# A hybrid RWKV-7/Mamba-2 step with a PEER layer: the mixer's triangular inverse on 64x64 blocks with a corner join, later k and r scores, and loop alignment without padding

## The chip, the cores and the metric

The kernel runs on one core of a Trainium2 chip. The metric is the device time of one execution in microseconds (us). The kernel before takes 2727.44 us, the median of 3 runs (2725.97 to 2730.17).

## The reference

One layer is applied to 576 tokens: 512 of a prompt and 64 of a sample stream, with a model width of 1024. `n = RMSNorm(x)`, `P = n @ W_in`; the columns of P go to eight RWKV-7 heads and eight Mamba-2 heads of 64 channels; `h = x + W_out [RWKV || Mamba]`; then `h = h + PEER(RMSNorm(h))`, and a last RMSNorm. The part that matters here is the RWKV recurrence, per head with a 64x64 state S:

```
def step(S, inp):
    r_t, w_t, k_t, v_t, a_t, b_t = inp
    sa = jnp.einsum('bhvk,bhk->bhv', S, a_t)
    S = S * w_t[:, :, None, :] + sa[..., None] * b_t[:, :, None, :] + v_t[..., None] * k_t[:, :, None, :]
    return S, jnp.einsum('bhvk,bhk->bhv', S, r_t)
```

PEER picks 128 experts for each token out of 16384 and applies them: `hid = x . u[e]`, `out = sum gelu(hid) * gate * v[e]`.

## The kernel before, in words

The program runs in stages: `project_in` (P), `mix` (both mixers), `project_out` and `route` (W_out, the expert keys and their ranking), `spread_gates` (gates as a dense table), `experts`, `finish`. Each stage is a block with one instruction stream for each engine, and the streams meet through semaphores. Names of engines in the profile: PE is TensorE, DVE VectorE, ACT ScalarE, POOL GpSimd, SP SyncE.

**The mixer** (`mix`, L593 to L1300). Tokens are taken in five tiles (`TILES`): four of 128 tokens, and the last of 64, the sample stream. In a tile the recurrence is solved in parallel form. A token's contribution `u` obeys (I - A) u = y, where A holds the scores a·b of every later token with every earlier one, strictly triangular, 128x128 for each of the eight heads. The kernel inverts the triangular matrix by doubling: level n (n = 1 to 6; 1 to 5 for 64 tokens, `last_level`, L524) joins diagonal blocks of 2^n into blocks of 2^(n+1). Heads are held in two halves e = 0, 1 of four heads q each, and for a half one level is:

- `q{n}{e}` (L859): four products of `mT` and `xx` (the inverse so far), 128x128 each.
- VectorE multiplies the bank by the level's mask into `pq` (L1239, tile name `level`).
- `x{n}{e}` (L865) and `t{n}{e}` (L866): four products each, `xt` with `pq` and `pq` with `xt`, the next inverse and its transpose; ScalarE copies the banks to `xx` and `xt` (`take`, L970; tile names `inv`, `invT`). On the last level only t is made.

A tile's steps are ordered by hand in `tile_parts` (L509). Every engine walks the same list and does what it has in each part; there is one order for each engine, and nothing overtakes. For a tile i the order is B1, L1, L2, ..., L6, B5, and between the levels stand parts of the next tile (A1 to A5, its preparation), of this tile's Mamba (Y1 to Y3) and of the tile before (C1 to C4, its output):

```
between = {1: ("C1", "Y1", "A1"), 2: ("C2", "A2", "Y2", "A2b"), 3: ("C3", "A3", "Y3"), 4: ("A4", "C4"), 5: ("A5",)}
```

B1 (L822 on TensorE) turns the four operands `bT`, `kT`, `aT`, `rT` and makes five pairs of scores (`scores`, L832): `ab` and `m` (the matrix and its transpose, which the levels need), then `ak`, `rb`, `rk`, which only B5 needs. VectorE in B1 (L1209 on): masks `ab` into `mT` and `m` into `xx` (L1220), adds the identity to `mT` and masks it into `xt`, half by half (L1229, L1230, SBUF to SBUF), then masks `ak` and `rb` (L1220). GpSimd adds the identity to `xx` (L1090), and masks `rk` (L1094), which ScalarE has copied. B5 (L892) makes y from the state and `ak`, u from y and `xt`, the output from `rb` and `rk`, and the new state; the next tile's B1 waits for that state.

Products go to eight PSUM banks in turn (`Banks`, L556, `mixer_jobs`, L529): a job may start when the job eight places ahead of it in the list has been taken. All numbers are four bytes wide; for one such product the trace holds two records of the weight load and two of the product.

In A3 VectorE does the key norm, `kk`, `tmp_a`, `b_hat` and `k_hat` (L1177 to L1183); in Y3 the Mamba state (L1265, L1267); in A4 eight operations on the Mamba segments (L1190) and a sum; in A1 ScalarE does a tanh and a sigmoid ahead of the products `w` and `a` (L780). GpSimd scales the outputs of the tile before in C3 (L718 to L722), makes the products of the bonus (L1079, L1080) and `xw` in A3, and does Mamba's norm in L5 (L1111).

**The experts** (`experts`, L1799). For TensorE each of 32 groups has 192 products for `hidden` (18 groups; the others were made ahead) and 192 for `out`, three products each with a split of the operands (`three_products`, L113). The groups are walked by `groups` (L1835 on): the first one, a loop over pairs, the 18th, and a second loop with seven turns of two groups. TensorE's stream alone is aligned: ahead of both loops stands `eng.addr_align(align)` (L1842, L1848) with `FETCH` = 256 instructions.

Of the kernel before, what the change touches and what calls it, by code (L numbers as in the profile page):

```python
# [32 lines left out]
P = 128  # L33
# [30 lines left out]
LEVELS = 7  # L64
# [14 lines left out]
C_MS, C_LT0, C_LEV = (P * n for n in range(6, 9))  # L79
C_DCOL = C_LEV + P * LEVELS  # L80
# [3 lines left out]
def shape_constants():  # L84
# [11 lines left out]
    c[:, C_MS:C_MS + P] = s < t  # L96
    for n in range(LEVELS):
        b = 1 << n
        m = ((s // (2 * b) == t // (2 * b)) & (s // b > t // b)) | (s == t)
        c[:, C_LEV + P * n:C_LEV + P * (n + 1)] = m if n else m & (s != t)  # L100
        if n == 0:
            c[:, C_LT0:C_LT0 + P] = m.T
# [406 lines left out]
def tile_parts():  # L509
    parts = [(name, 0) for name in ("A1", "A2", "A2b", "A3", "A4", "A5")]  # L510
    between = {1: ("C1", "Y1", "A1"), 2: ("C2", "A2", "Y2", "A2b"), 3: ("C3", "A3", "Y3"), 4: ("A4", "C4"), 5: ("A5",)}
    for i in range(NT):
        parts.append(("B1", i))
        for n in range(1, last_level(i) + 1):
            parts.append((f"L{n}", i))
            for name in between.get(n, ()):
                j = i + {"A": 1, "Y": 0, "C": -1}[name[0]]
                if 0 <= j < NT:
                    parts.append((name, j))
# [4 lines left out]
def last_level(i):  # L524

    return LEVELS - 1 if TILES[i][1] == P else LEVELS - 2


def mixer_jobs():  # L529
# [4 lines left out]
    for part, i in tile_parts():  # L534
# [6 lines left out]
                  + [(f"{name}{e}", "dve") for name in ("ab", "m", "ak", "rb") for e in range(2)]  # L541
                  + [("rk0", "act"), ("rk1", "act")],
# [3 lines left out]
        if part[0] == "L":  # L546
            n = int(part[1])
            one = [(f"q{n}{e}", "dve") for e in range(2)]
            for e in range(2):
                one += [(f"x{n}{e}", "act")] * (n < last_level(i)) + [(f"t{n}{e}", "act")]  # L550
# [42 lines left out]
def mix(core, params, om):  # L593
# [10 lines left out]
    with ExitStack() as ctx:  # L604
# [13 lines left out]
        mT, ak, rb, rk = (sb(n, P, 2, 4, P) for n in ("mT", "akT", "rbT", "rkT"))  # L618
        xx, xt = sb("inv", P, 2, 4, P), sb("invT", P, 2, 4, P)
        pq = sb("level", P, 2, 4, P)  # L620
# [103 lines left out]
        with nc.Block() as block:  # L724
# [25 lines left out]
            def _(pe):  # L750
                pe.wait_ge(par_in, 7 * 16)
                pe.wait_ge(zeroed, 3)
# [68 lines left out]

                def b1(i, tok, T, rc, xc):  # L822
# [9 lines left out]
                    def scores(name, lhs, rhs):  # L832
                        o = [b.start(pe, f"{name}{e}", i) for e in range(2)]
                        for q in range(4):
                            for e in range(2):
                                es = slice(e * HD, (e + 1) * HD)
                                ins = pe.matmul(o[e][0:T, q * T:(q + 1) * T], lhs[es, q, 0:T], rhs[es, q, 0:T],
# [4 lines left out]
                    scores("ab", bT, aT)  # L842
                    scores("m", aT, bT)
                    b.wait_taken(pe, "rT", i)
                    scores("ak", kT, aT)
                    scores("rb", bT, rT)
                    scores("rk", kT, rT)
# [1336 lines left out]
```

## Time and profile before

| what | us | busy share or clock |
|---|---|---|
| median of 3 runs | 2727.44 | |
| the profiled execution's own time | 2724.83 | |
| its span, first to last instruction | 2722.8 | mean clock 0.952 |
| TensorE busy in the span | 2509.6 | 92% |
| VectorE busy | 1550.2 | 57% |
| ScalarE busy | 968.2 | 36% |
| GpSimd busy | 651.8 | 24% |

How to read it: the profile is one execution, so the sum of a change is made against its own 2724.83 us. The clock is the share of full speed that TensorE was granted; it has two levels, 1.00 (2.4 GHz) and 0.50 (1.2 GHz), and what stands between is a mean over a stretch. A busy TensorE is not TensorE at its peak, since its records overlap. A number in brackets behind a row of the timeline is the time in which the engine stood idle just before, with what ended it.

### The profile page before, as it was taken

What the parts mean: (1) busy time and instruction counts of PE and PEld (TensorE: products, weight loads), DVE (VectorE), ACT (ScalarE), POOL (GpSimd) and SP (SyncE); (2) the same over time, 40 slices, a digit from 0 to 9 for tenths busy, and PEclk for the clock granted to TensorE, in tenths of its full rate; (3) what the DMA queues carried; (4) which work ended last, traced back from release to release, by engine and by line L of the source; (5) the groups of instructions that cost most, each with busy time, mean ns of one, the idle gap of its engine ahead of it and who ended that gap; (6) DMA issues with size and microseconds to landing.
All of it is one profiled execution on the core that took longest, in us unless ns stands there. A gap on an engine that the chain in (4) does not pass through costs nothing. (4 is left out here: it accounts for less than half of the span.)

```text
span 2722.8 us, 48234 instructions
## 1 busy us (share of the span) xinstructions
PE 2509.6 (92%) x18910; PEld 2446.0 (90%) x18910; DVE 1550.2 (57%) x2800; ACT 968.2 (36%) x1818; POOL 651.8 (24%) x313
## 2 busy tenths in 40 slices
PE   7977888887899899899979999999999998999997
PEld 6976778787799899888879999999999998999997
DVE  4334554633678776677745454454554543677774
ACT  3335334422332232688853322322322221222222
POOL 2433343423254545111122211211211210000000
PEclk9997899868999899999989999999999999999999
DMA  5331000003233233366664323323323322454551
GB/s 182 114 106 41 24 24 1 13 1 128 65 98 96 90 102 102 115 181 191 193 209 150 112 94 110 112 94 110 112 94 110 112 94 78 153 175 158 191 174 40
DMA packets 162452, 296.11 MB, mean 109 GB/s; under 512 B 11873, under 2 KB 99233, under 8 KB 158121
## 3 DMA queue, kind: packets, MB, share of 16 engines
q1 hardware_dynamic: 162344, 294.61, 32.9%
q8 instruction: 76, 1.25, 0.2%
q14 instruction: 32, 0.25, 0.0%
HBM read 230.26 MB, written 64.31 MB: 108 GB/s over the span
## 5 line engine op out<-in xcount | busy, mean ns | idle before, releaser
L115 PE MATMUL banks<-w_high,v_high 128*128 128x288 f32 x2048 | 605.4, 296 | 12.0 <-issue 11.6
L117 PE MATMUL banks<-w_high,v_low 128*128 128x288 f32 x2048 | 605.6, 296 | 0.0
L116 PE MATMUL banks<-w_low,v_high 128*128 128x288 f32 x2048 | 604.3, 295 | 0.0
L115 PE MATMUL banks<-res_hi,u_high 128*128 128x288 f32 x1440 | 428.6, 298 | 11.7 <-ACTq L2004 10.9
L117 PE MATMUL banks<-res_hi,u_low 128*128 128x288 f32 x1440 | 425.7, 296 | 0.0
L116 PE MATMUL banks<-res_lo,u_high 128*128 128x288 f32 x1440 | 425.4, 295 | 0.0
L115 PEld LDWEIGHTS banks<-w_high,v_high 128*128 128x128 f32 x2048 | 385.2, 188 | 15.5 <-issue 11.8
L117 PEld LDWEIGHTS banks<-w_high,v_low 128*128 128x128 f32 x2048 | 385.3, 188 | 0.0
L116 PEld LDWEIGHTS banks<-w_low,v_high 128*128 128x128 f32 x2048 | 385.2, 188 | 0.0
L1998 DVE TENSOR_TENSOR res_x<-banks,res_x 128x288 f32<-128x288 f32 x512 | 225.4, 455 | 280.7 <-PE banks L117 280.7
L1618 POOL TENSOR_TENSOR u_low<-u_raw,u_high 128x1024 fp32r<-128x1024 f32 x72 | 183.6, 2551 | 707.1 <-ACT u_high L1614 707.1
L1892 ACT ACTIVATE v_high<-v_raw 128x1024 fp32r<-128x1024 f32 x128 | 135.3, 1059 | 473.2 <-PE banks L117 473.2
L115 PE MATMUL banks<-res_hi,q_wh 128*128 128x288 f32 x864 | 263.0, 304 | 32.4 <-POOL q_wl L199 22.6
L1969 DVE TENSOR_TENSOR gated<-gelu_out,gates_in 128x576 f32<-128x576 f32 x128 | 156.7, 1224 | 226.6 <-ACT gelu_out L1949 226.6
L115 PEld LDWEIGHTS banks<-res_hi,u_high 128*128 128x128 f32 x1440 | 271.5, 189 | 12.2 <-issue 12.1
L116 PEld LDWEIGHTS banks<-res_lo,u_high 128*128 128x128 f32 x1440 | 271.5, 189 | 0.0
L117 PEld LDWEIGHTS banks<-res_hi,u_low 128*128 128x128 f32 x1440 | 271.3, 188 | 0.0
L116 PE MATMUL banks<-res_lo,q_wh 128*128 128x288 f32 x864 | 260.2, 301 | 0.0
L117 PE MATMUL banks<-res_hi,q_wl 128*128 128x288 f32 x864 | 260.0, 301 | 0.0
L1974 DVE TENSOR_TENSOR w_low<-gated,w_high 128x576 fp32r<-128x576 f32 x128 | 191.4, 1495 | 54.2 <-ACT w_high L1941 54.2
L115 PEld LDWEIGHTS banks<-res_hi,q_wh 128*128 128x128 f32 x864 | 167.7, 194 | 37.4 <-POOL q_wl L199 24.6
L1896 DVE TENSOR_TENSOR v_low<-v_raw,v_high 128x1024 fp32r<-128x1024 f32 x128 | 156.6, 1225 | 43.3 <-ACT v_high L1892 43.3
(327 smaller groups left out, 4473.5 us busy)
## 6 DMA issues: line engine op xcount, KB each, us to landing
v_raw<-arg_v SPq DMA_DIRECT2D x128, 512.0 KB, 3.9
scratch_gates<-gate_stage SPq DMA_DIRECT2D x18, 2048.0 KB, 9.3
u_raw<-arg_u SPq DMA_DIRECT2D x36, 1024.0 KB, 5.8
gates_in<-scratch_gates SPq DMA_DIRECT2D x32, 1152.0 KB, 7.2
q_raw<-arg_u SPq DMA_DIRECT2D x38, 512.0 KB, 3.6
scratch_hidden<-gelu_ahead SPq DMA_DIRECT2D x56, 288.0 KB, 2.4
gelu_out<-scratch_hidden SPq DMA_DIRECT2D x56, 288.0 KB, 2.9
in_raw<-arg_w_in SPq DMA_DIRECT2D x25, 512.0 KB, 4.0
```

What stands on the lines that cost most here:

```text
L115: pe.matmul(out, ah, bh, start=first, stop=False)
L116: pe.matmul(out, ah, bl, start=False, stop=False)
L117: return pe.matmul(out, al, bh, start=False, stop=last)
L1618: pool.tensor_tensor(self.lo[:, jj % 2], self.raw[:, jj // 2, jj % 2], self.hi[:, jj % 2].bitcast(F32), ALU.subtract).then_inc(self.low, 1)
L1892: act.activation(vh[:, q], v_raw[:, q], ACT.Copy).then_inc(v_high, 1)
L1896: dve.tensor_tensor(vl[:, q], v_raw[:, q], vh[:, q].bitcast(F32), ALU.subtract).then_inc(v_low, 1)
L1969: dve.tensor_tensor(prod[:, jj % 2, :], gelu[:, jj % 2, :], gates[:, par, :, jj], ALU.mult).then_inc(prod_done, 1)
L1974: dve.tensor_tensor(wl[:, par, jj, :], prod[:, jj % 2, :], wh[:, par, jj, :].bitcast(F32), ALU.subtract).then_inc(w_low, 1)
L1998: dve.tensor_tensor(x, core.psum[:, 4 + k % 4, 0:HALF], x, ALU.add).then_inc(out_added, 1)
```

## The change

It does five things.

1. The inverse is built on the two 64x64 diagonal blocks of each 128x128 matrix, up to level 5: `mT`, `inv` (with `inv[:, e, 0]` the inverse and `inv[:, e, 1]` its transpose) and `pq` hold 64 columns for each head, masks of the levels are 64 columns wide, and a product is made for each block. Tokens 0 to 63 lie on partitions 0 to 63, the others on 64 to 127.
2. x and t of a half share one bank and one copy of 512 elements (256 of each). On level 5 ScalarE copies the blocks to where they are needed in three pieces (`last_blocks`).
3. Level 6 becomes `join`: the corner scores `al` (tokens of the first half with tokens of the second), kept in `mL`, times the first block's inverse, copied, times the second block's transposed inverse, copied into the corner of `xt` by ScalarE. There are four products of 64x64 for each half in either step. `xt` is zeroed once, on GpSimd.
4. The scores `ak`, `rb` and `rk` with their masks become parts of their own, S1 behind level 1, S2 behind level 2, S3 behind level 3.
5. The first alignment in `experts` skips its padding by a branch (`max_nops=0`), the second is removed.

The core of the diff:

```diff
-LEVELS = 7
+LEVELS = 6
+HALF_T = 64
...
-    between = {1: ("C1", "Y1", "A1"), 2: ("C2", "A2", "Y2", "A2b"), 3: ("C3", "A3", "Y3"), 4: ("A4", "C4"), 5: ("A5",)}
+    between = {1: ("C1", "Y1", "S1", "A1"), 2: ("C2", "A2", "Y2", "A2b", "S2"), 3: ("C3", "A3", "Y3", "S3"),
+               4: ("A4", "C4"), 5: ("A5",)}
...
-    return LEVELS - 1 if TILES[i][1] == P else LEVELS - 2
+    return LEVELS if TILES[i][1] == P else LEVELS - 1
...
+                def blocks(name, i, T, lhs, rhs):
+                    o = [b.start(pe, f"{name}{e}", i) for e in range(2)]
+                    for q in range(4):
+                        for e in range(2):
+                            es = slice(e * HD, (e + 1) * HD)
+                            for d in range(T // HALF_T):
+                                ds = slice(d * HALF_T, (d + 1) * HALF_T)
+                                ins = pe.matmul(o[e][ds, q * HALF_T:(q + 1) * HALF_T], lhs[es, q, ds], rhs[es, q, ds],
+                                                start=True, stop=True)
+                            if q == 3:
+                                b.finish(ins)
+
+                def by_block(o, T, lhs, rhs, at=0):
+                    for q in range(4):
+                        for d in range(T // HALF_T):
+                            ds = slice(d * HALF_T, (d + 1) * HALF_T)
+                            ins = pe.matmul(o[ds, at + q * HALF_T:at + (q + 1) * HALF_T], lhs[ds, q, :], rhs[ds, q, :],
+                                            start=True, stop=True)
+                    return ins
...
-                            four(f"q{n}{e}", i, T, lambda q: mT[0:T, e, q, 0:T], lambda q: xx[0:T, e, q, 0:T])
+                            b.finish(by_block(b.start(pe, f"q{n}{e}", i), T, mT[:, e], inv[:, e, 0]))
                         for e in range(2):
                             b.wait_taken(pe, f"q{n}{e}", i)
-                            if n > 1:
-                                b.wait_taken(pe, f"t{n - 1}{e}", i)
-                            if n < last:
-                                four(f"x{n}{e}", i, T, lambda q: xt[0:T, e, q, 0:T], lambda q: pq[0:T, e, q, 0:T])
-                            four(f"t{n}{e}", i, T, lambda q: pq[0:T, e, q, 0:T], lambda q: xt[0:T, e, q, 0:T])
+                            o = b.start(pe, f"x{n}{e}", i)
+                            by_block(o, T, inv[:, e, 1], pq[:, e])
+                            b.finish(by_block(o, T, pq[:, e], inv[:, e, 1], 4 * HALF_T))
...
+                def join(i, tok, T, rc, xc):
+                    lo, hi = slice(0, HALF_T), slice(HALF_T, P)
...
+                    for e in range(2):
+                        b.wait_taken(pe, f"al{e}", i)
+                        b.wait_taken(pe, f"x{LEVELS - 1}{e}", i)
+                        four_blocks(f"q{LEVELS}", e, hi, lambda q: mL[:, e, q, :], lambda q: inv[lo, e, 0, q, :])
+                    for e in range(2):
+                        b.wait_taken(pe, f"q{LEVELS}{e}", i)
+                        four_blocks(f"x{LEVELS}", e, lo, lambda q: pq[hi, e, q, :], lambda q: xt[hi, e, q, hi])
...
+                def last_blocks(name, i, e, T):
+                    o = b.get(act, name, i)[:, :].rearrange("p (x q t) -> p x q t", x=2, t=HALF_T)
+                    if T == P:
+                        act.activation(inv[0:HALF_T, e, 0], o[0:HALF_T, 0], ACT.Copy)
+                    for d in range(T // HALF_T):
+                        ds = slice(d * HALF_T, (d + 1) * HALF_T)
+                        ins = act.activation(xt[ds, e, :, ds], o[ds, 1], ACT.Copy)
+                    b.took(ins, name, i)
...
                 if align:
-                    eng.addr_align(align)
+                    eng.addr_align(align, max_nops=0)
                 with eng.Fori(0, NH // 2 - 1) as it:
...
                 whole(eng, NH - 1, 1, first=False, last=True)
-                if align:
-                    eng.addr_align(align)
                 with eng.Fori(0, (NG - NH) // 2) as it:
```

## Rows read from the trace of the kernel before

**Rows 1.** Stretches: us, busy PE, PEld, DVE, ACT, POOL, clock, DMA, GB/s
```profile
200.00:620.00 420.00, 345.32 (x2847) 311.83 (x2847) 208.73 (x363) 164.12 (x301) 146.33 (x113) 0.82 0.07 20
...
1393.00:2722.00 1329.00, 1291.31 (x9650) 1284.49 (x9648) 718.84 (x907) 350.35 (x483) 183.59 (x72) 0.99 0.36 122
```

**Rows 2.** Timeline, third tile, first level: start, us, engine, line
```profile
395.36 1.16 PE L837 MATMUL banks<-a_hatT,b_hatT 64*128 64x128 f32 x16 [0.44 <-ACT a_hatT L970]
...
396.55 1.29 DVE L1220 TENSOR_TENSOR mT<-banks,shape_constants 128x512 f32<-128x512 f32 x2 [2.70 <-PE banks L837]
...
403.81 1.64 DVE L1230 TENSOR_TENSOR invT<-mT,shape_constants 128x512 f32<-128x512 f32 x1
...
408.49 2.08 PE L769 MATMUL banks<-level,invT 128*128 128x128 f32 x8 [0.90 <-DVE level L1239]
...
401.52 3.38 POOL L1094 TENSOR_TENSOR rkT<-rkT,shape_constants 128x512 f32<-128x512 f32 x2
...
413.74 0.70 PE L873 MATMUL banks<-ssm_states,xbc_in 64*128 64x256 f32 x4
```

**Rows 3.** Timeline of the last tile (64 tokens), first level
```profile
561.28 1.12 PE L837 MATMUL banks<-a_hatT,b_hatT 64*64 64x64 f32 x16
...
566.10 0.99 DVE L1230 TENSOR_TENSOR invT<-mT,shape_constants 64x256 f32<-64x256 f32 x1
...
568.80 1.11 PE L769 MATMUL banks<-level,invT 64*64 64x64 f32 x8 [0.96 <-DVE level L1239]
```

**Rows 4.** Timeline of the third tile, level 2
```profile
420.51 1.95 PE L769 MATMUL banks<-inv,mT 128*128 128x128 f32 x16
...
426.03 1.90 PE L880 MATMUL banks<-xdt,segments 128*128 128x64 f32 x16
```

**Rows 5.** Timeline of the third tile, levels 3 and 4
```profile
431.51 2.05 PE L769 MATMUL banks<-inv,mT 128*128 128x128 f32 x16
...
443.73 2.08 PE L769 MATMUL banks<-level,invT 128*128 128x128 f32 x8 [3.88 <-DVE level L1239]
...
449.99 1.95 PE L769 MATMUL banks<-shape_constants,dA_rows 128*128 128x128 f32 x16
```

**Rows 6.** Timeline: third tile's level 5 and B5, fourth tile's scores
```profile
454.56 1.16 PE L769 MATMUL banks<-level,invT 128*128 128x128 f32 x8 [0.40 <-DVE level L1239]
...
461.96 1.06 PE L899 MATMUL banks<-s_mid_pairs,a_hatT 128*128 128x128 f32 x8
...
479.21 1.47 PE L837 MATMUL banks<-a_hatT,b_hatT 64*128 64x128 f32 x16
```

**Rows 7.** Timeline: weight loads of half and quarter array at both clocks
```profile
467.76 0.55 PEld L910 LDWEIGHTS banks<-v_tok,k_hat 128*64 128x64 f32 x16
...
533.35 1.00 PEld L769 LDWEIGHTS banks<-shape_constants,dA_rows 64*64 64x64 f32 x16
...
579.84 1.82 PEld L769 LDWEIGHTS banks<-inv,mT 64*64 64x64 f32 x16
```

**Rows 8.** DVE groups by form: the level mask of 256 elements
```profile
L1239 DVE TENSOR_TENSOR level<-banks,shape_constants 64x256 f32<-64x256 f32 x10 | 4.1, 413 | 5.9 <-PE banks L769 5.8
```

**Rows 9.** Stretches of the tensor engine: us, busy (records), granted clock
```profile
380.00:385.00 5.00, 5.00 (x48) 1.00 0.01 3
...
560.00:565.00 5.00, 4.95 (x82) 0.50 0.01 3
...
565.00:570.00 5.00, 3.09 (x43) 0.84 0.00 0
...
575.00:605.00 30.00, 29.89 (x254) 0.50 0.01 1
```

**Rows 10.** Timeline of PE around the entry of the experts' second loop
```profile
2311.97 0.60 PE L115 MATMUL banks<-w_high,v_high 128*128 128x288 f32 x1 [11.57 <-issue]
...
2312.37 0.44 PE L116 MATMUL banks<-w_low,v_high 128*128 128x288 f32 x1
...
2312.61 0.44 PE L117 MATMUL banks<-w_high,v_low 128*128 128x288 f32 x1
```

More of the change, by code:

```diff
@@ L78 @@
 C_ID, C_ONE, C_TRI, C_REV, C_DINC, C_DEXC = (P * n for n in range(6))
-C_MS, C_LT0, C_LEV = (P * n for n in range(6, 9))
-C_DCOL = C_LEV + P * LEVELS
+C_MS = P * 6
+C_MSB, C_IDB, C_LTB, C_LEV = (P * 7 + HALF_T * n for n in range(4))
+C_DCOL = C_LEV + HALF_T * LEVELS
 C_N = C_DCOL + 2
@@ L547, in mixer_jobs @@
             n = int(part[1])
-            one = [(f"q{n}{e}", "dve") for e in range(2)]
-            for e in range(2):
-                one += [(f"x{n}{e}", "act")] * (n < last_level(i)) + [(f"t{n}{e}", "act")]
+            one = [(f"q{n}{e}", "dve" if n < LEVELS else "act") for e in range(2)]
+            one += [(f"x{n}{e}", "act") for e in range(2)]
             one += {1: [("yo0", "dve"), ("yo1", "dve")], 2: [("yd", "dve")], 3: [("st", "dve")]}.get(n, [])
@@ L617, in mix @@
         bT, kT, aT, rT = (sb(n, P, 4, P) for n in ("b_hatT", "k_hatT", "a_hatT", "r_hatT"))
-        mT, ak, rb, rk = (sb(n, P, 2, 4, P) for n in ("mT", "akT", "rbT", "rkT"))
-        xx, xt = sb("inv", P, 2, 4, P), sb("invT", P, 2, 4, P)
-        pq = sb("level", P, 2, 4, P)
+        ak, rb, rk = (sb(n, P, 2, 4, P) for n in ("akT", "rbT", "rkT"))
+        mT, mL = sb("mT_blocks", P, 2, 4, HALF_T), sb("mT_corner", HALF_T, 2, 4, HALF_T)
+        inv = sb("inv_blocks", P, 2, 2, 4, HALF_T)
+        xt = sb("invT", P, 2, 4, P)
+        pq = sb("level", P, 2, 4, HALF_T)
         s0d = sb("s_mid_pairs", P, 4, 2, HD)
@@ L830, in b1 @@
                     b.wait_taken(pe, "aT", i)
-                    def scores(name, lhs, rhs):
-                        o = [b.start(pe, f"{name}{e}", i) for e in range(2)]
+                    blocks("ab", i, T, bT, aT)
+                    blocks("m", i, T, aT, bT)
+                    if T == P:
+                        lo, hi = slice(0, HALF_T), slice(HALF_T, P)
+                        o = [b.start(pe, f"al{e}", i) for e in range(2)]
                         for q in range(4):
@@ L957, in c4 @@
                     outs("or", i, T, os_)
-                run_parts({"A1": a1, "A2": a2, "A4": a4, "B1": b1, "B5": b5, "C4": c4,
-                           **{f"L{n}": level(n) for n in range(1, LEVELS)}})
+                run_parts({"A1": a1, "A2": a2, "A4": a4, "B1": b1, "S1": s1, "S2": s2, "S3": s3, "B5": b5, "C4": c4,
+                           **{f"L{n}": level(n) for n in range(1, LEVELS)}, f"L{LEVELS}": join})
             @block.scalar
@@ L1041, in c4 @@
                     take("or", i, om[:, 0:4, tok:tok + T], 4 * T)
-                run_parts({"A1": a1, "A2": a2, "A4": a4, "B1": b1, "B5": b5, "C2": c2, "C4": c4,
-                           **{f"L{n}": level(n) for n in range(1, LEVELS)}})
+                run_parts({"A1": a1, "A2": a2, "A4": a4, "B1": b1, "S3": s3, "B5": b5, "C2": c2, "C4": c4,
+                           **{f"L{n}": level(n) for n in range(1, LEVELS)}, f"L{LEVELS}": join})
             @block.gpsimd
```

117 lines of the change are left out of this document (79 added, 38 removed).

## The prediction

> **What bounds the kernel now.** I read the stretches first, then the timeline of one tile of the mixer, then the entry of the experts' second loop, because the change touches only these two. [rows 1] give the mixer 420 us with TensorE busy 345 of them at a mean clock of 0.82, and the experts 1329 us with TensorE busy 1291. So the experts are TensorE from end to end, and any hole there is paid in full. In the mixer no engine is full; one has to see, stage by stage, which wait ends last.
>
> In the third tile's first level [rows 2] the score products start at 395.36, and the first product of the level's second half starts only at 408.49, released by a VectorE mask. In between VectorE works through a queue: two masks of 512 elements, four slow operations on SBUF beside GpSimd (the last ends at 405.45), then the masks of the two later score pairs (akT and rbT, again 1.29 us a pair), and only then the level's own masks. The 32 records that follow take until 413.74, most of them at the lower clock. Level 2 [rows 4] is TensorE work: 5.52 us from its first product to the next step's. Level 3 to the second half of level 4 takes 12.22 us [rows 5], and its last 3.88 us are a wait for VectorE, which has eight operations of the next tile's preparation to do. Level 4's second half takes 6.26 us, again slowly. Level 5's and 6's rest takes 7.40 us to B5, and B5 to the next tile's scores 17.25 us [rows 6].
>
> In the experts [rows 10] TensorE stands for 11.57 us ahead of the second loop's first product, put down to "issue": nothing it waits for. That is where the second alignment stands in the code. Behind it products start 0.24 us apart; the stretch as a whole has a record each 0.13 to 0.14 (9650 in 1329 us).
>
> **The change, part by part.** Price of a product on a 64x64 block. A four-byte product leaves two records. The only half-array row at the upper clock is 16 records of 64 weight columns whose halves alternate: 0.55 us, 34 ns each [rows 7]. At the lower clock 16 paired 64x64 records take about 0.85 us, 53 ns each (the next group starts 0.85 after the first; busy 1.12 with the drain) [rows 3]. Unpaired 64x64 blocks cost 1.00/16 = 62 ns at the upper and 1.82/16 = 114 ns at the lower clock [rows 7]. The blocks of the change alternate between both halves of rows and of columns, so I take 36 ns upper, 53 ns lower, with 27 (half of 53) and 62 as ends. A level has 96 such records (32 in q, 64 in x): 3.5 us, against 5.35 for 48 full ones (16 in 1.95 less the overlap, 1.78 to 1.87). A level mask is 0.41 instead of 0.69 us [rows 8].
>
> First level. Only ab, m and the corner scores stay ahead; masks, GpSimd's identity and the four SBUF operations work on 256 elements. The last tile does just that today: from its scores at 561.28 the last of these operations ends at 567.09, 5.81 us [rows 3]. With the two level masks at once (the two score pairs are behind the level now) the x products start after about 6.65 us instead of 13.13. They are 64 records: 2.3 us at 36 ns, so the step ends after 9.0 to 9.5 instead of 18.4. The ak scores now stand behind it (+1.0 us on TensorE, 16 records as at 395.36), though part of that covers the wait for ScalarE's tanh that follows. Net -8.8; the other three full tiles take 19 to 20 us there now, so -9.5 on average.
>
> Level 2: q 0.58 us for one half, drain 0.27 (1.12 less 0.85 [rows 3]), mask 0.41, then x 2.3: 3.64, so -1.9. The rb scores come behind A2, +1.0 on TensorE and 1.28 of masks ahead of level 3's on VectorE.
>
> Levels 3 and 4: VectorE's preparation ends last there, and it starts when level 3's masks are done. Shorter products move that start by about -1, the rb scores and masks by +1: zero. The cover of this zero is VectorE's queue itself; the rk scores (1.0) and the shorter level 3 lie under its 3.88 us wait. GpSimd's rk masks (3.38 us [rows 2]) go behind its share of the preparation and end before it has Mamba's norm to do. Level 4's second half: 2.3 to 3.4 instead of 6.26 here; two of the full tiles show some 6.4, two some 3.7. Mean -2.0.
>
> Level 5 starts 4.57 us behind that, bounded by VectorE's segments: -0.25. Then x (2.3), ScalarE's three copies a half, two corner products, each followed by a copy: 5.8 us to B5 instead of 7.4, so -1.6.
>
> A full tile: -9.5 - 1.9 - 0 - 2.0 - 0.25 - 1.6 = -15.25; four are -61. In tile 0 the rk masks meet SBUF operations that are alone today, +1. The last tile has its scores behind levels that are TensorE-bound at the lower clock (+0.85 three times), its level 5 makes both products of x (+1.7) and gains 1.2 at its first level: +3. Mixer at today's clock: -57. The zeroing of invT (1 us on GpSimd) and the smaller constants lie under the mixer's opening transfers: zero, 1 us if that cover went.
>
> The clock is the unknown. Today it stays at 1.00 through B5's products, which move 64 columns for 128 of weights (380 to 385 us, [rows 9]). Paired 64x64 work raised it (0.50, then 0.84 from 565), while 30 us of unpaired 64x64 work, TensorE busy throughout, left it at 0.50. The blocks of the change lie between these. Ends: no toll; or the lower level throughout, which costs 1.5 us a level and doubles what lies between. I take the lower level for about half the levels and what directly follows, 4 us a tile, 16 in all, nearer to the paired row than to the unpaired one. Mixer: -41.
>
> In the Trainium skill, the page TensorE: Matmul & The Clock Gate (Why this matters for your kernels) warns that thin matmuls make the clock oscillate. The rows at 560 to 570 show it rising and falling within ten microseconds, so here the warning holds in kind.
>
> Padding. The second alignment goes: -11.57. At the entry the products start 0.24 instead of 0.13 apart for some 4 us; without the stand the clock does not fall: -2. The first alignment's padding is hidden today, since this one stand is all that the page puts down to issue ahead of products: 0. Bounds for both: 0 if a fetch takes the padding's place, -15 if the first hid another. Taken: -13.6. From all, -41 - 13.6 = -54.6 on the profiled execution's 2724.8, which is 2.6 below the median of the runs: 2670.2 for such an execution, 2673 against the median of 2727.4.
>
> **Rivals.** (a) The blocks do not overlap: 62 ns a record, 6.0 us a level. First level -7.8, level 2 +0.4, level 4 -1.0, level 5 -0.25, join 0: -8.6 a tile, -35, last tile +3, padding -13.6: 2682. For it: nowhere do diagonal blocks run today. Against: both kinds of half alternate faster than that. The same page (Wait — 56ns, not 53.3ns?) says that the sequencer can spend about 62 ns on every matmul when hardware decoding is off. By that rule no alternation would help and this rival's time follows; the 34 ns row speaks against it.
>
> (b) Slower: the clock. If the lower level holds through levels and what lies between them, a tile pays up to 5 us in the levels and up to 29 in the rest (A1 6.8, A2 5.5, B5 17.25 [rows 2, 4 to 6], doubled at worst). The mechanism sits between level 2 and B5, where the work is thin and waits are many. It decides from a toll of (57 + 14)/4 = 18 us a tile; at 22 the result is 2745. For it: the last tile's 30 us at 0.50. Against: the full-size products between the levels.
>
> (c) The second loop, no longer on a boundary, pays at each of its seven turns what the padding cost once: up to 2 us each, which gives back the 14: 2686. Against: no loop turn shows a hole today.
>
> (d) The change does not reach what bounds: the moved masks queue on VectorE and GpSimd ahead of preparation, 5 us a tile more: 2693.
>
> **How the numbers follow.** Forecast with a toll of 0 to 8 us a tile: 0.72, 2657 to 2689. (a) 0.07, (c) 0.08, (d) 0.07, (b) 0.06, half of it slower. The likeliest gives 2673; the range goes from the toll-free clock with blocks at 27 ns a record (some 6 us more), 2651, to 2704, which takes in (a), (c), (d) and small cases of (b). A measurement of this kernel tells about 0.2%, 5.5 us, from no change: faster 0.94, same 0.03, slower 0.03.
>
> **What would show it.** In the changed profile: the first x product some 6.7 us behind the first scores, released by the level mask; a level 2 of 3.6 to 5.1 us; an unchanged 11 to 12 us from level 3 to level 4's second half, ended by VectorE; about 5.8 us from level 5's x to B5; no stand at the second loop's entry. Records of 53 ns and a mixer clock well under 0.82 would be the toll; 62 ns at the upper clock would be (a); seven holes at the loop's turns would be (c). A mixer shorter than 350 us or longer than 400 would prove the sum wrong.

## The result, and the profile after

The changed kernel takes 2650.48 us (median of 4 runs, 2646.44 to 2654.49) against 2727.28: a ratio of 0.9717 [0.97, 0.9734]. That is 76.8 us less, where 54.6 were forecast, and half a microsecond below the low end of the range. The profiled execution takes 2649.54 us with a span of 2647.6. Against the execution before the span fell by 75.2 us. The mixer gave 60.4 of it, read from where TensorE's first long stand behind `spread_gates` begins (1395.01 before, 1334.58 now), and the experts 14.8.

The stretches of both kernels, first before and then after (us, busy of TensorE, its loads, VectorE, ScalarE, GpSimd, then the clock). Of each kernel the first row runs from tile 0's B1 to the last tile's B1, the second from there to the last tile's B5. The third and fourth row of after answer to [rows 1]:

```profile
226.65:559.29 332.64, 282.49 (x2312) 257.13 (x2313) 176.76 (x296) 136.46 (x243) 120.10 (x87) 0.88 0.05 13
559.29:596.01 36.72, 34.65 (x349) 32.68 (x349) 17.63 (x39) 10.73 (x27) 15.08 (x14) 0.55 0.01 2
```

```profile
225.62:496.14 270.52, 222.68 (x3464) 196.26 (x3465) 146.10 (x288) 119.58 (x235) 110.56 (x87) 0.88 0.06 16
496.14:535.74 39.60, 36.13 (x365) 34.68 (x365) 17.87 (x39) 9.13 (x19) 16.48 (x16) 0.52 0.01 1
200.00:570.00 370.00, 289.03 (x4029) 255.76 (x4030) 184.85 (x362) 152.12 (x295) 141.01 (x116) 0.80 0.10 29
1333.00:2647.60 1314.60, 1288.44 (x9647) 1282.08 (x9645) 718.51 (x907) 350.20 (x483) 183.54 (x72) 0.99 0.36 124
```

The four full tiles lost 62 us at the same mean clock, 0.88. The forecast had expected the clock to fall. A mean of 0.88 is 24% of the time at 0.50, so TensorE stood at the lower level for some 80 us of these tiles before and for some 65 after (worked out from the two rows).

Third tile, first level, in the timeline of after, against [rows 2]:

```profile
360.93 0.91 PE L850 MATMUL banks<-a_hatT,b_hatT 64*64 64x64 f32 x32
...
361.89 0.76 DVE L1236 TENSOR_TENSOR mT_blocks<-banks,shape_constants 128x256 f32<-128x256 f32 x2 [3.67 <-PE banks L850]
...
365.11 1.12 PE L859 MATMUL banks<-inv_blocks,mT_blocks 64*64 64x64 f32 x16 [2.34 <-POOL inv_blocks L1174]
366.23 0.43 DVE L1318 TENSOR_TENSOR inv_blocks<-mT_blocks,shape_constants 128x256 f32<-128x256 f32 x1
...
367.64 1.09 PE L859 MATMUL banks<-level,inv_blocks 64*64 64x64 f32 x16
...
371.22 0.92 PE L917 MATMUL banks<-ssm_states,xbc_in 64*128 64x256 f32 x4
```

From the scores to the first x product it takes 6.71 us where 13.13 stood before, and 10.29 to the step's end instead of 18.38. The last SBUF operation ends at 366.66, 5.73 behind the scores (5.81 were read from the last tile). Here the x products run at the lower clock, 3.58 us for 64 records and their drain.

The same tile behind it: level 2, the wait ahead of level 4's second half, level 5's second half, and B5 (against [rows 4 to 6]):

```profile
378.08 1.15 PE L859 MATMUL banks<-inv_blocks,mT_blocks 64*64 64x64 f32 x32
379.29 0.68 PE L859 MATMUL banks<-level,inv_blocks 64*64 64x64 f32 x16
...
381.30 1.22 PE L924 MATMUL banks<-xdt,segments 128*128 128x64 f32 x9
...
387.78 1.15 PE L859 MATMUL banks<-inv_blocks,mT_blocks 64*64 64x64 f32 x32
...
399.00 1.12 PE L859 MATMUL banks<-level,inv_blocks 64*64 64x64 f32 x16 [4.62 <-DVE level L1236]
399.91 1.06 PE L859 MATMUL banks<-inv_blocks,level 64*64 64x64 f32 x16
400.76 1.06 PE L859 MATMUL banks<-level,inv_blocks 64*64 64x64 f32 x16
...
402.55 2.05 PE L780 MATMUL banks<-shape_constants,dA_rows 128*128 128x128 f32 x16
...
406.95 0.68 PE L859 MATMUL banks<-level,inv_blocks 64*64 64x64 f32 x16 [0.84 <-DVE level L1236]
...
412.06 1.56 PE L960 MATMUL banks<-s_mid_pairs,a_hatT 128*128 128x128 f32 x8
```

The price of a record is in the queue of weight loads. Groups of 16 follow each other in level 2 at the upper clock:

```profile
379.29 0.54 PEld L859 LDWEIGHTS banks<-level,inv_blocks 64*64 64x64 f32 x16 [0.20 <-DVE level L1236]
379.75 0.55 PEld L859 LDWEIGHTS banks<-inv_blocks,level 64*64 64x64 f32 x16
```

A group starts 0.46 us after the one before: 29 ns a record. Half of the 16 records are in either quarter of the array, so within one quarter they are 58 ns apart (0.46 us for 8), and the two quarters run side by side. At the lower clock, in level 4 of this tile, the groups start 0.85 us apart (399.91, 400.76): 53 ns, as taken from [rows 3].

Step by step, from starts in the timeline, mean of the four full tiles, change in us:

| step | forecast | measured |
|---|---|---|
| level scores to level 1's end | -9.5 | -9.1 |
| level 2 | -1.9 | -2.3 |
| level 2's end (with rb's scores) to level 4's second half | 0 | -0.2 |
| level 4's second half | -2.0 | -2.0 |
| from there to level 5's second half | -0.25 | -0.2 |
| level 5's second half and join, to B5 | -1.6 | -2.4 |
| B5 to the next tile's scores | 0 | +0.55 |
| toll of a lower clock on all of these | +4 | (in the rows above) |
| a full tile | -11.25 | -15.65 |
| the last tile, scores to B5 | +3 | +3.3 |

### The profile page after: what moved, and what is told of

The parts are those of the page before. It is cut to its first block and busy times, and to the rows that moved or that the text cites. A ratio compares the mean times of both kernels' runs of the same rounds, so it can differ in the third digit from the quotient of the medians.

```text
span 2647.6 us, 50323 instructions
## 1 busy us (share of the span) xinstructions
PE 2449.5 (93%) x20078; PEld 2386.9 (90%) x20078; DVE 1520.1 (57%) x2792; ACT 949.3 (36%) x1802; POOL 642.8 (24%) x314
```

## The experiments

Each ratio is taken against runs of the kernel before made beside the experiment's own; their medians lie between 2725.7 and 2729.9 us. Where kernels of different groups of runs are compared, 4 us of a difference between medians can come from that, and the ratios are the better measure. The smaller blocks, the shared copy and the corner join (parts 1 to 3 of the change) were not run apart: what each gave is read from the table only.

**The padding alone, and the mixer alone.** The kernel before with the two edits of the experts, and the changed kernel with the two alignments as they were:

```diff
-                    eng.addr_align(align)
+                    eng.addr_align(align, max_nops=0)
...
-                if align:
-                    eng.addr_align(align)
```

> The kernel before with only the two alignment edits. Theory A (the padding in front of the second loop is executed and costs its whole stand, and the slow products behind it are its consequence): the 11.57 us stand and the 2 us behind it go, and about 1 us at the first loop's entry, so -13.6 to -15 us, ratio 0.9948. Rival B (a loop that starts off a boundary pays at each of its seven turns): holes of 1 to 2 us appear at the turns of the second loop and the ratio is 0.998 to 1.000.

Measured: 2715.61 us (2710.56 to 2716.27), ratio 0.9949 [0.9933, 0.9966]. In the profile the experts are 14.8 us shorter than before, as with the whole change, and none of the seven turns shows a hole. The profiled execution as a whole is 9.2 us shorter only, because its mixer, the same program as before, took 5.7 us longer; the medians are 12.1 apart.

> The changed kernel with both alignments as before. Theory A (the gain is the sum of two separate stages): -60 to -62 us, ratio 0.9775, mixer stretch as in the changed kernel, and the stand of some 12 us is back before the second loop. Rival B (part of the gain was only a place of code or a favourable clock in the profiled execution): less than 50 us.

Measured: 2669.44 us (2661.78 to 2680.24), ratio 0.9776 [0.9756, 0.9796]. The two parts, -12.1 and -58.2, make 70.3 of 76.8, and what is missing is less than the spread of the mixer: these four runs lie 18.5 us apart, where seven of the kernel before lie within 3.2. The profiled one has this stretch, from B5 of tile 0 to the next B1; the changed kernel's own stretch, with the same records, stands in the second fence:

```profile
279.34:302.23 22.89, 20.63 (x118) 19.94 (x117) 1.28 (x4) 2.77 (x5) 0.71 (x1) 0.50 0.00 1
```

```profile
277.68:291.06 13.38, 11.12 (x118) 10.67 (x117) 1.28 (x4) 2.66 (x5) 0.87 (x1) 1.00 0.01 1
```

118 records either way, 9.5 us apart, for the clock alone. Between the two kernels nothing in the mixer differs. The profile of the kernel with the last tile filled (below), whose full tiles are again the same program, has the long one too:

```profile
279.58:302.47 22.89, 20.63 (x118) 19.93 (x117) 1.28 (x4) 2.77 (x5) 0.63 (x1) 0.50 0.00 1
```

So the mechanism of rival (b) exists. From B5 to the next scores it cost 10.7 us at the most (26.5 where the upper clock takes 15.75), against the 17.25 that the rival gave as its worst, and it struck this stretch in two of four profiles of these tiles; behind the third tile all four show some 5 us of it or none (20.7 to 20.8, once 15.75).

**Blocks that do not alternate.** In `by_block` all four products of a block follow each other before the other block's:

```diff
-                    for q in range(4):
-                        for d in range(T // HALF_T):
+                    for d in range(T // HALF_T):
+                        for q in range(4):
```

> The changed kernel with the order of the block products turned round: the four products of the first diagonal block, then the four of the second, instead of one of each in turn. Same products, same number of records. Theory A (the two diagonal blocks run side by side only when they alternate, and their double use of the array is what keeps the clock up): records 62 ns apart at the upper clock instead of 29, levels fall to the lower clock and 106 to 114 ns there as in the last tile; level 2 from 3.2 to 5.5 us or more, total +40 to +100 us against the changed kernel. Rival B (small products are cheap by themselves, the order does not matter): within 3 us of the changed kernel.

Measured: 2658.63 us (2657.76 to 2659.99), ratio 0.9746 [0.973, 0.9762], some 8 us over the changed kernel, which neither expectation named. Level 2 of the third tile in its timeline:

```profile
391.69 1.54 PE L859 MATMUL banks<-inv_blocks,mT_blocks 64*64 64x64 f32 x32
393.17 0.79 PE L859 MATMUL banks<-level,inv_blocks 64*64 64x64 f32 x13
393.75 0.27 PE L859 MATMUL banks<-inv_blocks,level 64*64 64x64 f32 x1
393.80 0.22 PE L859 MATMUL banks<-level,inv_blocks 64*64 64x64 f32 x1
393.85 0.22 PE L859 MATMUL banks<-inv_blocks,level 64*64 64x64 f32 x1
393.86 0.22 PE L859 MATMUL banks<-level,inv_blocks 64*64 64x64 f32 x1
...
395.79 0.88 PE L924 MATMUL banks<-xdt,segments 128*128 128x64 f32 x6
```

The level takes 4.10 us instead of 3.22. Its groups of 16 start 0.58 us apart (393.17, 393.75), 36 ns a record, and where one product's second block meets the next one's first, their records mix (393.75 to 393.86). Inside a run of four products in one quarter the records are 58 ns apart here too (393.80, 393.86), close to rival (a)'s 62. But the end of each run overlaps with the start of the next one in the other quarter, and that brings the mean down to 36. Alternation is worth 7 ns a record, not the 26 between the price taken and that of rival (a).

**The last tile filled.** The last tile has one block. Here it makes both products; those of the second block work on what the tile before left and nobody reads them:

```diff
-                        for d in range(T // HALF_T):
+                        for d in (1, 0) if T == HALF_T else (0, 1):
```

> The changed kernel with the level products of the last tile (64 tokens, one block) made for both blocks, the second one on what the tile before left there and read by nobody. Twice the products in the last tile's levels. Theory A (alternating blocks overlap and raise the clock): the added products cost nothing, the clock rises from 0.50 in the last tile's levels, and its 38 us from scores to B5 shrink by 8 to 17 us. Rival B (the clock answers to something else, such as how often TensorE waits): same clock 0.50, same time within 2 us. Rival C (they don't overlap at the lower clock): +20 us or more.

Measured: 2643.61 us (2634.25 to 2652.87), ratio 0.9684 [0.9652, 0.9717]. The runs spread over 18.6 us and the interval reaches into that of the changed kernel, so these totals alone do not show a gain. The last tile:

```profile
505.95:539.49 33.54, 25.96 (x604) 24.60 (x604) 16.84 (x39) 9.15 (x19) 15.70 (x15) 0.80 0.01 3
```

239 records more than in the changed kernel and 6 us less, with the clock at 0.80 instead of 0.52: from its scores to B5 32.0 us against 38.1, a gain of 6 where theory A had 8 to 17. The other profiles say how far one may trust this: with one block the last tile stands at 0.52 to 0.71 and takes 34.0 to 38.1 us, with both blocks at 0.74 to 0.95 and 30.6 to 33.1 (30.6 with its first wait filled too). The stages behind it gain as well, 794.3 us from its B5 to the experts' first long stand instead of 798.8.

In the Trainium skill, TensorE: Matmul & The Clock Gate (Why this matters for your kernels) warns of a clock that oscillates under thin products. The full tiles bear that out, with their blocks in pairs: in the third one the x products of levels 1 and 4 run at the lower clock, those of levels 2 and 5 at the upper. The last tile of the changed kernel, on one block, does not oscillate but stays at the lower level nearly throughout (0.52).

**The changed kernel again**, to see how much of all this is one execution's luck.

> The changed kernel again. Its four runs so far lie between 2646.4 and 2654.5 us, and the kernel with the change in the mixer alone, whose mixer is the same program, between 2661.8 and 2680.2, 18.4 us apart. Theory A (where TensorE's clock falls within a tile is not fixed by the program; it differs from one execution to the next): the runs here spread over 10 us or more, around 2651, and the profile shows falls at other places than the first one did. Theory B (the program fixes them, and the padding in the experts explains the rest): within 4 us of 2650.5, with the same falls.

Measured: 2653.28 us (2646.49 to 2659.07), ratio 0.9727 [0.9709, 0.9746]. Nine runs of the changed kernel now lie between 2646.4 and 2659.1, where the 13 of the kernel before shown with these two lie within 5.6. In this profile level 1's x products of the second and fourth tile take 1.99 us, where they took 3.18 and 3.59 in the first one; the third tile's take 3.43 in one and 3.58 in the other. Theory A holds. The page TensorE: Matmul & The Clock Gate of the Trainium skill (What's actually happening) says as much, that one kernel measures different numbers of slow matmuls in different runs; the two profiles agree with it.

**The idle time filled.** On top of the filled last tile, products of the identity, read by nobody, stand in three waits of the full tiles:

```diff
+                        if n == 0 and i in (1, 2, 3):
+                            filler(o, 5)
                         pe.wait_ge(hats, 4 * i + n + 1)
...
+                            if n == 1 and e == 0 and T == P:
+                                filler(b.start(pe, f"q{n}{e}", i), 8)
...
+                            if n == 4 and e == 0 and i in (1, 2, 3):
+                                filler(b.start(pe, f"x{n}{e}", i), 16)
                             b.wait_taken(pe, f"q{n}{e}", i)
```

> The last tile filled as before, and in the full tiles products of the identity that nobody reads, put into waits of TensorE: 5 (1.1 us) ahead of the wait for the next tile's operands, 8 (1.8 us) ahead of level 1's wait for GpSimd, 16 (3.5 us) ahead of level 4's wait for VectorE. Theory A (the clock falls behind these waits, so the waits cost more than their length): the low stretches of tiles 0 to 3, 43 us in the first profile after and 69 us in the last experiment, shrink to under 30 us, and the time is 3 to 10 us under the kernel with the last tile filled alone (2643.6), 2634 to 2641, with a narrower spread. Theory B (the falls come from thin products, not from the waits): no shrinking, and 0 to 3 us slower than 2643.6 where a filler outlasts its wait.

Measured: 2634.08 us (2633.2 to 2637.28), ratio 0.9654 [0.9641, 0.9667]. Level 4 of the third tile:

```profile
390.54 1.15 PE L863 MATMUL banks<-inv_blocks,mT_blocks 64*64 64x64 f32 x32
391.62 3.84 PE L785 MATMUL banks<-ident 128*128 128x128 f32 x32
396.33 0.68 PE L863 MATMUL banks<-level,inv_blocks 64*64 64x64 f32 x16 [0.87 <-DVE level L1246]
...
398.34 0.94 PE L780 MATMUL banks<-shape_constants,dA_rows 128*128 128x128 f32 x6
```

VectorE still ends the wait, but the 64 records behind it take 2.01 us, and took 3.55 in the changed kernel. The first level, scores to end, takes 8.08 us in each of the three later tiles, 9.3 to 10.3 without the fillers. This is the table's missing toll: the changed kernel pays it, the kernel before paid it too, and so it hardly shows in the difference. The total lies clear of the changed kernel's, but not of that of the last tile filled alone (the intervals overlap); what the full tiles' fillers bring is read from the last experiment. The four full tiles at a clock of 0.93, and the last one:

```profile
226.89:491.68 264.79, 233.98 (x3655) 207.35 (x3655) 145.65 (x288) 119.05 (x235) 110.65 (x87) 0.93 0.06 17
491.68:526.79 35.11, 27.52 (x605) 25.87 (x605) 16.76 (x39) 9.42 (x19) 16.56 (x16) 0.74 0.01 3
```

**The scores where they were.** In the changed kernel, S1 to S3 straight behind B1:

```diff
-        parts.append(("B1", i))
+        parts += [(name, i) for name in ("B1", "S1", "S2", "S3")]
```

> The changed kernel with the ak, rb and rk scores straight behind the level's own, as before: the blocks without the move. Theory A (the move takes VectorE's queue and TensorE's products off the first level): four masks of 0.65 us stand ahead of level 1's masks again, of which the present wait of 2.3 us for GpSimd covers some 1.5, and three score pairs of 1.0 us stand on TensorE ahead of level 1; from the level scores to level 1's end a full tile takes 11.5 to 13 us instead of 10.1, level 2 to 3 gives 1.0 back, so the time is 2 to 8 us over the changed kernel, 2653 to 2659. Theory B (the smaller blocks alone bring the first level): within 2 us of the changed kernel.

Measured: 2649.54 us (2648.51 to 2651.09), ratio 0.9711 [0.9696, 0.9726], theory B. The third tile's first level, and the end of its wait in level 4:

```profile
367.06 0.73 PE L849 MATMUL banks<-a_hatT,b_hatT 64*64 64x64 f32 x32
...
371.53 1.15 PE L858 MATMUL banks<-inv_blocks,mT_blocks 64*64 64x64 f32 x32
...
374.55 0.68 PE L858 MATMUL banks<-level,inv_blocks 64*64 64x64 f32 x16 [1.87 <-DVE level L1235]
...
376.56 0.70 PE L916 MATMUL banks<-ssm_states,xbc_in 64*128 64x256 f32 x4
...
404.37 1.12 PE L858 MATMUL banks<-level,inv_blocks 64*64 64x64 f32 x16 [7.18 <-DVE level L1235]
```

The first level ends 9.50 us behind its scores, at the upper clock, 1.4 more than the moved scores allow (8.08). But the score products fill the wait for GpSimd instead of lengthening later steps, and level 4's wait for VectorE, now 7.18 us, starts from a shorter level 2 to 3. The sum of the masks on VectorE is the same, and VectorE ends that wait. And the move loses at the clock what it gains in the queue: without it level 1's x products take 2.01 us in each of the four full tiles, with it 3.2 to 3.6 in the first profile and in two tiles of the second, behind a wait for GpSimd in which TensorE has nothing to do. From the scores to level 4's second half the third tile takes 37.3 us here and 38.1 in the changed kernel. With the small blocks the move is worth nothing that can be measured.

**The scores alone moved.** The kernel before with S1, S2 and S3 as parts of their own behind levels 1 to 3:

```diff
-    between = {1: ("C1", "Y1", "A1"), 2: ("C2", "A2", "Y2", "A2b"), 3: ("C3", "A3", "Y3"), 4: ("A4", "C4"), 5: ("A5",)}
+    between = {1: ("C1", "Y1", "S1", "A1"), 2: ("C2", "A2", "Y2", "A2b", "S2"), 3: ("C3", "A3", "Y3", "S3"),
+               4: ("A4", "C4"), 5: ("A5",)}
```

> The kernel before with the ak, rb and rk scores moved behind levels 1 to 3 and nothing else. Theory A (VectorE's queue ahead of the level's masks bounds the first level): two masks of 1.29 us a pair leave the path, the first level takes 16 to 17 us instead of 19.2, rb's scores give 1.0 back behind level 2 and level 4's wait takes what is left; a full tile gains 1 to 2.6 us and the time is 2717 to 2724 against 2727.5. Theory B (the levels' products at 128x128 bound it, or the masks queue ahead of the preparation and come back there): 2725 to 2730.

Measured: 2710.87 us (2706.01 to 2717.51), ratio 0.9942 [0.9923, 0.9962]: 16 us by the ratio and 19 by the medians, where theory A had 3 to 10. Third tile, first level:

```profile
389.42 1.16 PE L830 MATMUL banks<-a_hatT,b_hatT 64*128 64x128 f32 x16
...
396.26 2.02 PE L772 MATMUL banks<-inv,mT 128*128 128x128 f32 x8 [4.78 <-POOL inv L1101]
...
400.01 1.06 PE L772 MATMUL banks<-level,invT 128*128 128x128 f32 x8
...
403.67 0.70 PE L882 MATMUL banks<-ssm_states,xbc_in 64*128 64x256 f32 x4
```

The first x product comes 10.59 us behind the scores: the 2.6 us of masks that the prediction named. The x products then take 3.66 us at the upper clock where [rows 2] have 5.25, more than half of it at the lower. So on full blocks the profile shows the move paying twice. In the four full tiles, 16.5 us shorter together, the steps up to the first x product and those behind them as far as level 4 make some 6, which is what theory A expected; the other 10 are the same products at a higher clock. How much of those 10 belongs to the move and how much to this execution is open: it is the fastest of four that lie 11.5 us apart.

**The filler ahead of the fence.** The 5 products had landed behind TensorE's wait for VectorE's state and delayed the operands. Here 6 stand ahead of it, in every tile but the first, and the last tile's first wait is filled as well:

```diff
+                    if i > 0:
+                        filler(b.start(pe, "bT", i), 6)
                     b_fence(pe, i)
...
-                        if n == 0 and i in (1, 2, 3):
-                            filler(o, 5)
...
-                            if n == 1 and e == 0 and T == P:
+                            if n == 1 and e == 0:
```

> The kernel with the idle time filled, with the first filler (6 products of the identity, 1.3 us) moved ahead of the wait for VectorE's state, in which TensorE stood 1.57 us anyway, for all tiles behind the first, and the last tile's wait for GpSimd filled as well. Theory A (the filler behind that wait only delayed the next tile's operands by 1.1 us): 3 tiles give 1.1 us back, and the clock falls less in the last tile: 2628 to 2632 against 2634.1. Theory B (the wait's length is set by VectorE, which the filler did not touch, and other falls take the place of these): 2633 to 2637.

Measured: 2628.71 us (2623.93 to 2638.18), ratio 0.9642 [0.9621, 0.9663]. The turn from tile 0 to tile 1, first in the kernel of the experiment before, then here:

```profile
290.93 2.47 PE L785 MATMUL banks<-ident 128*128 128x128 f32 x10 [1.58 <-DVE state_tmp L1380]
293.19 1.06 PE L875 MATMUL banks<-ident,b_hat 128*128 128x128 f32 x4
```

```profile
288.84 1.60 PE L785 MATMUL banks<-ident 128*128 128x128 f32 x12
290.48 0.63 PE L875 MATMUL banks<-ident,b_hat 128*128 128x128 f32 x4
```

The filler now covers the wait, and the operands follow it at the upper clock. The median fits theory A, but the runs spread over 14 us again and the intervals of the two kernels overlap, so that this one is faster than the last is not shown. It is the lowest median of all.

**The paddings one at a time**, each put back into the kernel with the idle time filled.

```diff
-                    eng.addr_align(align, max_nops=0)
+                    eng.addr_align(align)
```

> The kernel with the idle time filled (2634.1 us, 4 us of spread), and ahead of the experts' first loop the alignment with its padding, as before; the second stays away. Theory A (the first padding cost the 1.1 us at that loop's entry which is in the trace of before and not in that of after): 2634.5 to 2636. Theory B (it was hidden): 2633.5 to 2634.5. Theory C (its padding depends on where the code ends, and can be as long as the second's): up to 2646.

Measured: 2649.18 us (2644.95 to 2652.54), ratio 0.9713 [0.97, 0.9726], 15 us more by the medians and 16 by the ratios. TensorE at the entry of the first loop:

```profile
1360.57 0.29 PE L123 MATMUL banks<-res_hi,u_low 128*128 128x288 f32 x1
1371.33 0.58 PE L121 MATMUL banks<-res_hi,u_high 128*128 128x288 f32 x1 [10.47 <-issue]
1371.71 0.44 PE L122 MATMUL banks<-res_lo,u_high 128*128 128x288 f32 x1
```

Theory C: with the fillers' instructions in front of it, the first alignment, which cost at most 1.1 us in the kernel before, stands 10.47 us. That it stands because of a longer padding is inferred from the code; padding instructions leave no record.

```diff
+                if align:
+                    eng.addr_align(align)
                 with eng.Fori(0, (NG - NH) // 2) as it:
```

> The kernel with the idle time filled, and ahead of the experts' second loop the alignment with its padding, as before; the first stays without padding. Theory A (a stand of 11.7 us and 2.0 us of products at the lower clock behind it): 13.7 us more, 2646.5 to 2649. Theory B (the length of the padding depends on where the code in front of it ends, which differs here): anything from 0 to 14 us more, with a stand at the second loop's entry as long as the difference less 2 us where the clock falls.

Measured: 2646.34 us (2642.66 to 2654.01), ratio 0.9708 [0.9691, 0.9724], 12.3 us more by the medians and 14.7 by the ratios. The entry of the second loop:

```profile
2235.00 0.60 PE L121 MATMUL banks<-w_high,v_high 128*128 128x288 f32 x1 [11.58 <-issue]
```

11.58 us, as in [rows 10], with slow products behind it; the experts take 14.3 us more than without it. Theory A.

**The last tile not filled**, the full tiles' idle time filled:

```diff
-                        for d in (1, 0) if T == HALF_T else (0, 1):
+                        for d in range(T // HALF_T):
```

> The kernel with the idle time of the full tiles filled, and the last tile as in the changed kernel, its products for one block only. Theory A (both fillers earn: the full tiles' some 8 us, the last tile's some 6): 2638 to 2643, last tile at the lower clock throughout and 36 to 38 us from its scores to B5 against 33. Theory B (the last tile's filler alone made the difference, and the full tiles' only narrowed the spread): 2645 to 2651.

Measured: 2643.46 us (2638.57 to 2643.6), ratio 0.9687 [0.9674, 0.9701]. So the last tile's filler is worth 9 us by the medians and the full tiles' 7 to 10, against the changed kernel's two medians; the interval here lies clear of the changed kernel's second set of runs and touches that of the first. The profiles show less for the last tile: 2.2 us in the tile (33.5 with the filler, in the two experiments on the paddings) and some 4.8 behind it. The last tile is at 0.71 here, not at 0.50 throughout as expected:

```profile
493.86:529.61 35.75, 28.55 (x364) 27.03 (x364) 17.07 (x39) 9.14 (x19) 16.56 (x16) 0.71 0.01 2
```

## Why the prediction was right in kind and short by 22 us

- **The failed step is the clock's toll**, "the lower level for about half the levels and what directly follows, 4 us a tile, 16 in all", put on top of a mixer of -57 "at today's clock". The mixer measured -60.4 with everything in it, so nothing is left of the 16 as an addition: the four full tiles stand at 0.88 before and after. The argument compared the new blocks with two pieces of the last tile and asked how low they would hold the clock. It left out that the full tiles before were at the lower clock for about a quarter of their time already, in part behind the same waits for VectorE and GpSimd.
- **How large the toll is in either kernel** can be estimated by setting each step against the same step at the upper clock in another tile or profile. For the changed kernel: first level 10.1 us in the mean where it takes 8.08 (8.6 in tile 0), level 4's second half to level 5's 7.2 where it takes 6.4, B5 to the next scores 17.2 where it takes 15.75 (14.9 ahead of the last tile). That is some 17 us in four tiles. For the kernel before: level 1's x products 5.7 where they take 3.67, then 9.4 where 8.25 (7.4 in the fourth tile), 16.6 where 15.65, some 18 us. So 16 was a fair size for what the new code pays; the error was to add it to a kernel that paid as much. It is also no constant: the four profiles with these full tiles give 267 to 285 us for them, which by this estimate puts the toll between 14 and 32.
- **The sum of -57 was not all at one clock**, and that hid a second error. Its x products were priced at the upper clock, while stretches that the change does not touch kept their old times, with the old toll in them (some 7 us). At the upper clock the new steps are also shorter than sized, by some 12 us in four tiles. The price of a record is part of that: 36 ns at the upper clock were taken, 29 measured, 0.45 us on 64 records, seen in level 2 (-2.3 for -1.9) and behind level 5 (-2.4 for -1.6). These two are the room in which a toll of 17 us could be paid and the sum still come out at -60.4. They are estimates from one profile each.
- **The first level** came at -9.1 for -9.5, and in part that is luck: the forecast took 9.0 to 9.5 us for it at the upper clock, where it takes 8.08, and the lower clock put 2 us back. The x products stand 6.1 us behind the scores at the upper clock and 6.7 in the third tile of the profile. That the moved scores carry 2.6 us of it is right on full blocks and wrong on the small ones, where moving them back cost nothing in the total. Only an experiment that undid them alone could show that.
- **Levels 3 and 4** came out at the predicted zero: the wait for VectorE ended last in both, and what TensorE saved there grew the wait from 3.88 to 4.62 us. Level 4's second half, -2.0, and the last tile, +3.3 for +3, were right.
- **The padding** gave 14.8 us in the experts for 13.6. The stand and the slow products behind it were right; 1 us more went at the first loop's entry, where the trace of before has a gap of 0.81 us put down to ScalarE.
- **The signs that it named** came in part: records of 53 ns in levels 1 and 4, but a mixer clock of 0.80 where 0.82 stood, and a mixer of some 360 us, inside the 350 to 400 outside of which the sum was to be wrong. So these bounds did not catch the error.
- **The rivals.** (a) fell: 29 ns alternating, 36 without; one quarter alone does run at 58, near its 62, but the quarters overlap. (c) fell: no turn of the loop shows a hole. (d) fell: VectorE's queue took the moved masks without a longer step. (b) had a real mechanism, seen in a stretch of 22.89 us in two profiles and smaller ones in others, but not in each tile, and the kernel before pays for it too. (Its 5 us for the levels do not follow from its own 1.5 us a level, which give 7.5 for five levels.)
- **The sum without the toll**, -57 and -13.6, would have given 2657 against the median, and some 5 us less with the records at 29 ns, 2652. Of the 20.6 us by which the profiled execution missed the forecast, 16 are the toll's term, 3.4 the rest of the mixer and 1.2 the padding; the median lies 1.6 further off. The range's low end was built from the toll-free sum with records of 27 ns, so it left no room below it.

## What to carry to other kernels

A change of the clock is a difference: before a toll is put on the new code, count in the trace how much of the old code ran at the lower level, and behind which waits, and price every step, changed or not, at one and the same clock. Where TensorE waits two to five microseconds for a vector engine inside thin work, products that nobody reads can be worth more than they cost; here the fillers of full and last tiles together brought 16 to 20 us. That they should stand ahead of the wait and be shorter than it is a likely reading of one turn in one profile; the totals do not show it. An alignment with padding cost between nothing and 11.6 us here, as far as one can infer by what code stood in front of it, so an edit far ahead of it can move 10 us; the branch over the padding showed no stand in any profile.

## What had not been expected of the hardware

- Records of products on 64x64 blocks that alternate between opposite quarters start 29 ns apart at the upper clock and 53 at the lower, and 58 ns apart inside one quarter at the upper clock. In the Trainium skill, TensorE: Matmul & The Clock Gate (Wait — 56ns, not 53.3ns?) gives the sequencer some 62 ns for each matmul without hardware decoding. Counted per record, 29 ns speak against it here; counted per product of two records, 58 ns lie just below it, and no run here tells which way it is counted.
- The same 118 records took 13.38 us in two profiles and 22.89 in two others, in the same code of the mixer, by the clock alone (1.00 and 0.50).
- The first loop's alignment, with its padding in both, shows no gap over 0.6 us in the kernel with the mixer alone changed, and 10.47 us with the fillers, which stand in code that runs more than 800 us earlier. That its padding differs in length is inferred, not seen.
